# Last stage of a decoder trunk: the output turned over chunk by chunk inside the gate stage, and stored in pieces of 512 bytes

## What is computed

```python
def run_trunk(h, p, ...):
    for i in range(DEPTH):
...
        h = h + rmsnorm(swiglu(rmsnorm(h, norm_g[i, 2]), w_gate[i], w_up[i], w_down[i]), norm_g[i, 3])
        h = h + jax.nn.sigmoid(h @ w_ple_gate[i]) * (p[i] @ w_ple[i])
    return h, ...
```

## Time and profile before

| | us |
|---|---|
| device time, three runs | 3348.18, 3350.90, 3351.05 |
| median | 3350.9 |
| the profiled execution's own time | 3350.36 |
| its span, first to last instruction | 3348.7 |

### The profile page before, as it was taken

The page is one execution under the profiler, slowest core; times in us unless marked ns, Lnnn a source line. Parts: engine busy times, 40 slices in busy tenths (PEclk is TensorE's granted clock), DMA queues, the critical chain, the costliest instruction groups (busy, mean ns, idle before and its releaser), DMA issues.

```text
span 3348.7 us, 52790 instructions
## 1 busy us (share of the span) xinstructions
PE 3148.7 (94%) x20520; PEld 2993.1 (89%) x20520; DVE 1602.6 (48%) x2736; ACT 863.8 (26%) x1547; POOL 229.7 (7%) x301
## 2 busy tenths in 40 slices
PE   7999999999999997999988998989899999999887
PEld 6999989999999996999987775459899999999887
DVE  5443265444444466443334555442644444444752
ACT  3111342111111122322234553333411111111221
POOL 1000010000000000000024441110100000000000
PEclk9999999999999998999999999999999999999998
DMA  2111101111111111113137556861111111111201
GB/s 87 44 44 44 46 26 51 45 45 45 45 45 45 45 58 32 38 38 124 61 94 159 108 103 250 331 218 39 38 45 45 45 45 45 45 45 45 64 26 60
DMA packets 232966, 239.17 MB, mean 71 GB/s; under 512 B 18661, under 2 KB 190693, under 8 KB 232754
## 3 DMA queue, kind: packets, MB, share of 16 engines
q1 hardware_dynamic: 208770, 155.74, 15.7%
q0 software_dynamic: 23984, 80.30, 8.2%
HBM read 201.11 MB, written 18.10 MB: 65 GB/s over the span
## 4 chain that ended last, share of the span: by engine, by line
PE 87%; DVE 6%; ACT 3%; issue 2%; DMA 1%; POOL 0%; DVEq 0%; ACTq 0%; POOLq 0%
PE psum L1828 20%; PE psum L1830 20%; PE psum L1829 20%; PE psum L1854 5%; PE psum L1848 5%; PE psum L1849 4%; PE psum L2262 2%; PE psum L2307 2%; PE psum L2246 2%; PE psum L2231 1%; PE psum L2326 1%; PE psum L2356 1%; PE psum L2232 1%; DMA q_high<-fsum_scratch 1%; DVE y L1187 1%
## 5 line engine op out<-in xcount | busy, mean ns | idle before, releaser
L1828 PE MATMUL psum<-xs_hi,w_hi 128*128 128x384 f32 (+1 forms) x2784 | 911.6, 327 | 15.3 <-DVE w_lo L1156 8.8
L1830 PE MATMUL psum<-xs_hi,w_lo 128*128 128x384 f32 (+1 forms) x2784 | 909.1, 327 | 0.0
L1829 PE MATMUL psum<-xs_lo,w_hi 128*128 128x384 f32 (+1 forms) x2784 | 908.5, 326 | 0.0
L1828 PEld LDWEIGHTS psum<-xs_hi,w_hi 128*128 128x128 f32 x2784 | 523.6, 188 | 18.0 <-issue 9.3
L1829 PEld LDWEIGHTS psum<-xs_lo,w_hi 128*128 128x128 f32 x2784 | 523.8, 188 | 0.0
L1830 PEld LDWEIGHTS psum<-xs_hi,w_lo 128*128 128x128 f32 x2784 | 523.5, 188 | 0.0
L1830 PE MATMUL psum<-hid_hi,w_lo 128*128 128x384 f32 (+1 forms) x1056 | 346.0, 328 | 0.0
L1829 PE MATMUL psum<-hid_lo,w_hi 128*128 128x384 f32 (+1 forms) x1056 | 345.1, 327 | 0.0
L1828 PE MATMUL psum<-hid_hi,w_hi 128*128 128x384 f32 (+1 forms) x1056 | 344.7, 326 | 0.0
L1525 DVE TENSOR_TENSOR y<-y,psum 128x384 f32<-128x384 f32 x528 | 269.0, 530 | 153.3 <-PE psum L1830 153.3
L712 ACT ACTIVATE w_hi<-raw 128x1024 fp32r<-128x1024 f32 x188 | 197.8, 1052 | 545.4 <-DVEq L1172 527.6
(11 more groups left out here) (291 smaller groups left out, 3752.1 us busy)
## 6 DMA issues: line engine op xcount, KB each, us to landing
kpage<-in_cache_k SPq DMA_DIRECT2D x64, 512.0 KB, 7.0
v_page<-in_cache_v POOLq DMA_DIRECT2D x64, 512.0 KB, 5.7
raw<-in_w_gate SPq DMA_DIRECT2D x44, 512.0 KB, 3.7
raw<-in_w_up SPq DMA_DIRECT2D x44, 512.0 KB, 3.7
raw<-in_w_down SPq DMA_DIRECT2D x44, 512.0 KB, 3.6
raw<-in_w_in SPq DMA_DIRECT2D x24, 512.0 KB, 3.6
raw<-in_w_ple_gate SPq DMA_DIRECT2D x16, 512.0 KB, 3.6
out<-rows_out POOLq DMA_DIRECT2D x16, 512.0 KB, 2.9
```

What stands on the lines that cost most here:

```text
L1828: M(out, wh, xh, start=first, stop=False)
L1829: M(out, wh, xl, start=False, stop=False)
L1830: return M(out, wl, xh, start=False, stop=last)
```

## The change

The output is turned over by feature chunk, inside the gate stage of layer 1. After tile `t` of gate chunk `m` (`m` from 1 to 6) PE turns over tile `t` of chunk `m - 1`: three transposes into bank 6 or 7 in turns (`chunk_rows`). In the last gate chunk two such groups stand behind each tile: tiles 0 and 1 of chunk 6 behind tile 0, tile 2 of chunk 6 and tile 0 of chunk 7 behind tile 1, tiles 1 and 2 of chunk 7 behind tile 2. The ninth block takes the last 128 tokens, so that it overlaps the eighth. ACT alone copies the three squares (128 x 384) into `yrow`, two buffers in the memory of `y`. POOL stores chunks 0 to 6, each with one DMA of 1024 pieces of 512 bytes for the prompt and one of 64 pieces for the sample tokens; of chunk 7 SP stores the prompt part in three DMAs, one a tile (384, 384 and 256 pieces), and POOL the sample part. DVE has no part in the output any more. The old output behind the stage is gone.

```diff
+    yrow = [sb(f"yrow{i}", [P, NTB, P], F32, A_Y + 4608 * i) for i in range(2)]
...
+        def y_block(tb):
+            return min(tb * P, T - P)
...
+        def y_rows_of(m, b0, b1):
+            return y_prompt[0, b0 * P:b1 * P, m * P:(m + 1) * P].rearrange("(b p) d -> p b d", p=P)
...
+        def y_sample_of(m):
+            return y_sample.rearrange("b t d -> (b t) d")[:, m * P:(m + 1) * P]
...
 (SP)
             ple(1)
+            for t, b1 in enumerate((3, 6, 8)):
+                sp.wait_ge(y_rows, NT * (C - 1) + t + 1)
+                sp.dma_start(y_rows_of(C - 1, 3 * t, b1), yrow[(C - 1) % 2][:, 3 * t:b1, :]).then_inc(last_stored, 16)
...
 (POOL)
             ffn(1)
-            store_rows(TR_Y, y_prompt[0], y_sample.rearrange("b t d -> (b t) d"))
-
-            pool.wait_ge(rows_stored[0], 16 * (NTB + 1))
-            pool.wait_ge(rows_stored[1], 16 * NTB)
+            for m in range(C - 1):
+                pool.wait_ge(y_rows, NT * (m + 1))
+                pool.dma_start(y_rows_of(m, 0, 8), yrow[m % 2][:, 0:8, :]).then_inc(y_stored[m % 2], 16)
+                pool.dma_start(y_sample_of(m), yrow[m % 2][P - NS:P, 8, :]).then_inc(y_stored[m % 2], 16)
+            pool.wait_ge(y_rows, NT * C)
+            pool.dma_start(y_sample_of(C - 1), yrow[(C - 1) % 2][P - NS:P, 8, :]).then_inc(last_sample_stored, 16)
...
+            for r in range(2):
+                pool.wait_ge(y_stored[r], 32 * ((C - r) // 2))
+            pool.wait_ge(last_stored, 16 * NT)
+            pool.wait_ge(last_sample_stored, 16)
...
 (ACT)
+                def chunk_rows(m, t):
+                    act_e.wait_ge(y_tr, NT * m + t + 1)
+                    if m > 1 and t == 0:
+                        act_e.wait_ge(y_stored[m % 2], 32 * (m // 2))
+                    A(yrow[m % 2][:, 3 * t:3 * t + 3, :], psum[:, 6 + (NT * m + t) % 2, 0:3 * P]
+                      .rearrange("p (b d) -> p b d", b=3), ACT.Copy).then_inc(y_rows, 1)
...
                         A(act[:, t0:t0 + n], acc(b0 + 2 * m + 1, t), ACT.Sigmoid).then_inc(ple_sig, 1)
+                        if layer == 1 and 0 < m < C - 1:
+                            chunk_rows(m - 1, t)
+                        if layer == 1 and m == C - 1:
+                            for k in ((6, 7), (8, 9), (10, 11))[t]:
+                                chunk_rows(C - 2 + (k - 6) // NT, k % NT)
...
-            act_e.wait_ge(ple_added, 2 * C * NT)
-            for tb in range(NTB):
-                row(TR_Y, tb)
...
 (DVE)
-            dve.wait_ge(ple_added, 2 * C * NT)
-            for tb in range(NTB):
-                row(TR_Y, tb)
...
 (PE)
                         ins.then_inc(acc_ready, 1)
+                        if layer == 1 and m < C - 1:
+                            chunk_rows(m - 1, t)
+                        elif layer == 1:
+                            for k in ((6, 7), (8, 9), (10, 11))[t]:
+                                chunk_rows(C - 2 + (k - 6) // NT, k % NT)
+
+            def chunk_rows(m, t):
+                k = NT * m + t
+                pe.wait_ge(ple_added, NT * (C + m) + t + 1)
+                if k == 0:
+                    pe.wait_ge(rb_used, STEP0["n_ffn1"] + NT)
+                elif k > 1:
+                    pe.wait_ge(y_rows, k - 1)
+                for j in range(3):
+                    b0 = y_block(3 * t + j)
+                    ins = nc.tensor.transpose(psum[:, 6 + k % 2, j * P:(j + 1) * P], h[:, m, b0:b0 + P], ident[:, :])
+                ins.then_inc(y_tr, 1)
...
-            pe.wait_ge(ple_added, 2 * C * NT)
-            pe.wait_ge(acc_free, ACCS + NT * BLKS)
-            transposes_in(TR_Y, out_of(h))
```

More of the change, by code:

```diff
@@ L288, in trunk @@
         ple_added = sem("ple_added")
+        y_tr, y_rows = sem("y_tr"), sem("y_rows")
+        y_stored = [sem(f"y_stored{i}") for i in range(2)]
+        last_stored, last_sample_stored = sem("last_stored"), sem("last_sample_stored")
         kT_stored = sem("kT_stored")
@@ L323, in trunk @@
         block = ctx.enter_context(nc.Block())
-        TR_X, TR_K, TR_V, TR_Y = 0, NTB, 2 * NTB, 3 * NTB
-        ROWS0 = {TR_K: 0, TR_V: NTB - 8, TR_Y: NTB + 1}
+        TR_X, TR_K, TR_V = 0, NTB, 2 * NTB
+        ROWS0 = {TR_K: 0, TR_V: NTB - 8}
         QBS = (7, 6, 1, 0, 5, 4, 3, 2)
@@ L686, in _ @@
             ffn(1)
-            store_rows(TR_Y, y_prompt[0], y_sample.rearrange("b t d -> (b t) d"))
-            pool.wait_ge(rows_stored[0], 16 * (NTB + 1))
-            pool.wait_ge(rows_stored[1], 16 * NTB)
+            for m in range(C - 1):
[4 more added lines that the diff above has]
+            pool.dma_start(y_sample_of(C - 1), yrow[(C - 1) % 2][P - NS:P, 8, :]).then_inc(last_sample_stored, 16)
+            pool.wait_ge(rows_stored[0], 16 * 5)
+            pool.wait_ge(rows_stored[1], 16 * 5)
+            for r in range(2):
+                pool.wait_ge(y_stored[r], 32 * ((C - r) // 2))
+            pool.wait_ge(last_stored, 16 * NT)
+            pool.wait_ge(last_sample_stored, 16)
             pool.wait_ge(conv_stored, 32)
@@ L2207, in _ @@
             transposes_in(TR_V, out_of(vT))
-            pe.wait_ge(tr_act, TR_Y)
-            pe.wait_ge(tr_dve, TR_Y)
+            pe.wait_ge(tr_act, TR_V + NTB)
+            pe.wait_ge(tr_dve, TR_V + NTB)
             pe.wait_ge(mask_ready, 2)
```

## The result

| | us |
|---|---|
| kernel before, four runs beside it | 3349.80 median (3348.18 to 3351.05) |
| changed kernel, four runs | 3330.65 median (3329.85 to 3332.45) |
| ratio | 0.9944, 95% interval 0.9927 to 0.9961 |
| profiled execution of the changed kernel | 3332.45, span 3330.8 |

The change gains 19.2 us, where I had forecast 10.8. The direction was right, and so was the mechanism in the gate stage; the error is at the very end of the program. Two executions in later batches, one of b1_sp (12764 us) and one of the kernel before (9240 us), ran in a slow state; they count in no ratio and move their medians by under 0.2 us.

A forecast was written before the change was run, and what follows sets the result against it. The output was taken as bound by two row buffers and store landings behind the last matmul. Removing 18.7 us there and adding 7.9 us of transposes gains 10.8: forecast 3340.1 us, 8-in-10 range 3337.5 to 3345.

The forecast's parts named there:

- What bounds the kernel: Output behind the gate stage: bound by two row buffers and the landing of stores, with no matmul beside it.
- Transposes, 7.9 us: Gate-stage matmul stream: 66 transposes at 0.099 us plus 20 places at 0.07 add 7.9 us; bounds 6.5 to 11.
- Rival (a): Gate-stage transposes exposed at their full 0.273 us each, 18.0 us in all, leaving a gain of 0.7; chance 0.05.
- Waits on PE, ACT hidden: Gate stage: transpose groups never wait for adds or copies; ACT's 24 copies of 0.49 us fit between sigmoids.
- Stores: Gate-stage chunk stores of 1024 pieces land in 4 us, range 2.8 to 10.4, and hold nothing up.
- Rival (b): Chunk stores land slowly, setting the end from 8.1 us; chance 0.04 for 8 to 19 us, 0.03 for slower kernel.
- The new end: Last landing 5.5 us behind E, the last sigmoid's start, instead of 24.2: 18.7 us removed, 17.2 to 18.8.
- The 7.9 us behind the last landing: From last landing to span's end: POOL's last waits, barrier, program's end; 7.9 us, taken as the same in both kernels.
- Rival (c): Program's end grows by 4 us or more, or overlooked waits cost 6; gain 4.5 to 7; chance 0.07 with another rival.

The follow-up runs named there:

- b1_sp: The kernel before with its nine row stores at the end issued by SyncE instead of GpSimd; median 3345.13 us, ratio 0.999.
- b3_nine: The kernel before with nine row buffers for the output instead of two, so no copy waits for a store; median 3343.78 us, ratio 0.9985.
- s4_double: The changed kernel with every output transpose made twice into the same place, six in a group instead of three; one run, 3341.59 us.
- b5_flush7: The kernel before with seven GpSimd loads of 1024 pieces of 512 bytes into unused memory in the gate stage; median 3345.81 us, ratio 0.9986.
- b7_drain: The kernel before with one additional GpSimd DRAIN in the gate stage, ahead of its nine row stores; median 3343.09 us, ratio 0.998.
- s5_drain: The changed kernel with one additional GpSimd DRAIN behind chunk 5's stores; median 3330.48 us, ratio 0.9941.
- b2_late: The kernel before with 60 additional transposes that hold GpSimd for 8 us ahead of its end, all stores landed; one run, 3359.01 us.
- s1_all_sp: The changed kernel with all stores of the last stage issued by SyncE, GpSimd only waiting; median 3335.72 us, ratio 0.9961.

## Why the prediction was wrong in size

By its own steps:

- **What bounds the kernel**: right. The chain of copies and landings was the end, and with more buffers (b3_nine) or quicker landings (b1_sp) it shortened as read.
- **Transposes, 7.9 us**: 7.34 measured, inside the bounds (6.5 to 11), so the term was 0.56 too large. I had 0.099 for each and 0.07 for each place; the doubled groups say 0.111 for each and about nothing for a place. The chunk period forecast as 15.9 is 15.81 (3290.35 to 3306.16). Rival (a), 0.273 each and no gain, is refuted by this sum and by s4_double.
- **Waits on PE, ACT hidden**: right. PE is busy for all 99.28 us, ACT for 21.
- **Stores**: 3.7 us where I took 4. Rival (b) is refuted: no store of the last stage took over 4.7 us to land, and the chunk stores would count from 8.1.
- **The new end**: the sum was E + 5.5 for the last landing, the trace has E + 4.85. GpSimd issues 0.28 behind the copy, not 0.55 (the rows that I cited give 0.51). In the kernel before each store has a wait of its own ahead of it, for the second engine, and the issue comes 0.52 behind that (3337.40 and 3337.92 for the last); here the store waits for one semaphore and has no such instruction, which is the likely reason. SyncE issues after 0.02. Both kinds of last store land in 1.8 us instead of 2.2 and 2.6. Counted to the DRAIN, 24.34 became 5.28: 19.06 removed, where I had 18.7.
- **The 7.9 us behind the last landing**: this is the step that failed. "I take them as the same in both kernels" had no row behind it and no bound. 7.5 of the 7.9 were GpSimd's DRAIN, and it fell to 2.6, since with the seven chunk stores of 1024 pieces in the gate stage 66 older DMAs no longer count at the end; seven loads of the same pieces do the same with the old output (b5_flush7). Rival (c) had the place, a change in those 7.9 us, and only the wrong sign: it let them grow.

The miss adds up from the profiled executions: 4.90 from the DRAIN, 0.56 from the transposes, 0.36 from the end, 5.82 of 16.62 - 10.8. The other 2.5 us up to the 19.2 between medians are S, 1.32 earlier, which no part of the change explains, and the place of the profiled executions among their runs.

The lesson for the working: the stretch taken as fixed was 7.9 us, three quarters of the forecast gain. A stretch in which no row says what is done needs ends like any unknown cost, here 0 and 7.9 on the side of gain; the low end of the range would then have been 3329.6.

**Open.** What sets off the clearing was not settled; the limit may be in pieces. By length at 81.7 ns about 91 DMAs counted in the kernel before and 31 in the changed one, 15 of these the last stage's own. And the clearing was only seen as its effect, a shorter DRAIN and perhaps a late issue; nothing in the trace shows it by itself.

## What to carry to other kernels

- Read what stands behind the last landing, too: in these kernels GpSimd's closing DRAIN cost 82 ns for each of its DMAs that was not cleared before, with all engines waiting. An earlier DRAIN on GpSimd while it was idle took 6.7 us off the end of a kernel, for nothing on the path (b7_drain). In the changed kernel, where 2.3 us were left to win, the same showed in the profile and not in the median (s5_drain).
- Transposes of 128 x 128 float32 squares in a full matmul stream cost 0.11 us each here, whether in threes or sixes. Output that becomes final piece by piece can be turned over and stored beside the product, if the copies and the stores have room there; what is left behind the last piece should be small and its stores short (1.8 us for 128 KB or 32 KB).

## What was unexpected in the hardware

GpSimd's DRAIN: 40 ns with no DMA behind the last DRAIN, 298 with 3, 777 with 9, and 9136 for the kernel with 20 more where before had 7500; 81.7 to 81.8 ns for each more or less in three pairs of kernels. GpSimd loads that nobody needed made a kernel faster (b5_flush7: DRAIN 7500 to 2682). 8 us of waiting did not shorten it (b2_late).

SyncE's 512 KB stores of 512-byte pieces took 4.3 us to land and GpSimd's 3.7 (s1_all_sp and after), but SyncE issues the next thing sooner behind a copy, 0.02 against 0.28 us.
